# Down products of one-expert units as three rounded products, and scatters signalled by result buffer, in a hybrid trunk step with a 64-expert mixture

## The chip, the cores and the metric

One core of one Trainium2 chip. The metric is the device time of one execution of the whole program in microseconds (us), the median of several runs.

## The reference, cut to what matters

One inference step of one transformer-like layer over 384 tokens (128 context, 256 latent) of width 1024: input projections, three mixers (attention, convolution, recurrence), an output projection, and a mixture of experts. The change lies in the mixture:

```python
def moe(x, lp):
    s = jax.nn.sigmoid((x @ lp['w_router']).astype(jnp.float32))
    ...
    _, eidx = lax.top_k(jnp.where(emask, sel, NEG_BIG), TOP_K)     # 8 of 64 experts a token
    w = w / jnp.sum(w, axis=-1, keepdims=True) * ROUTED_SCALE
    ...
    hg = jnp.einsum('nd,edf->nef', x, lp['w_gate'])                # 1024 -> 256
    hu = jnp.einsum('nd,edf->nef', x, lp['w_up'])
    hid = jax.nn.silu(hg) * hu * combine[:, :, None]
    y = jnp.einsum('nef,efd->nd', hid, lp['w_down'])               # 256 -> 1024
    sh = (jax.nn.silu(x @ lp['w_sh_gate']) * (x @ lp['w_sh_up'])) @ lp['w_sh_down']
    return y + sh
```

All data are float32. Each expert has 1 MB (1024 KB) of gate weights, 1 MB of up weights and 1 MB of down weights.

## The kernel before

The program is written engine by engine: each engine has its own stream of instructions and waits on counting semaphores (`x.wait_ge(sem, n)`), which other engines' instructions or landed DMAs raise. The order of the work on every engine is thus written out by hand.

**The mixture in units.** After the router, the program makes a table of rounds. A *unit* is a pass of up to 128 token rows: either one expert with 128 rows (slots 0 and 1), or two experts with 64 rows each (slot 2, whose second expert lies in slot 3). Units come in the order one expert, one expert, two experts, and again; for these inputs there are 40, so 27 have one expert and 13 two. Their number is known only on the chip, so each engine runs a loop of `PASSES` passes over `BODY` = 12 written-out steps, each under an `If(i <= units)`. In the code, `p` is the place in the pass, `p % 3` the slot, `p % 2` the half of double buffers.

**Four weight slots** (`WSLOT`) each hold gate and up weights (`GU_W`, 128x4096) and down weights (`DN_W`, 128x2048). SyncE refills the gate and up part of a slot once the unit's gate and up products are done (`gu_ready`), the down part once its down products are (`dn_ready`), lines 658 to 663.

**A step `i`**, by engine:

- *TensorE* (lines 1995 to 2069): transposes the gathered rows of the unit after next (`transposes`, L2002), multiplies the first half of gate and up of the next unit (L2016, or L2018 and L2019 for two experts), transposes the hidden of this unit (`hidden_t`, L2051), makes the index products of a later unit (L1671), the second half of gate and up, and then this unit's down products into banks 6 and 7 of PSUM (`down`, L2033, or L2035 and L2036). Before the down products it waits for `ht_done` and `ys_done` (the banks' last content taken).
- *ScalarE* (`step`, from line 990): copies transposed rows out of PSUM (`take_xt`, L979), copies the transposed hidden (`HT`, L996), and does the silu of the next gate products (`silu`, L983).
- *VectorE* (`step`, from line 1590): makes one-hots of a later unit (L1120, L1121) and its row indices from the index products (L1130, L1131), multiplies silu and up products (`hidden`, L1577), and scales the down products by the routing weight into one of two result buffers (`YS`, L1599), for which it waits for `added`.
- *GpSimd* (`step`, from line 1074): gathers the token rows of a later unit into one of three buffers by an indirect DMA (`gather`, L1052), then writes the result rows of this unit to `y_parts` in memory by an indirect DMA (L1083), the *scatter*. Then it waits until that scatter has landed and raises `added`:

```python
indirect_dma_start(y_parts, ..., YS[:, p % 2, :], ...).then_inc(scat, 16)
pool.wait_ge(scat, 16 * i)
pool.sem_inc(added, 1)
```

Before the loop, GpSimd multiplies and adds the shared expert's outputs (`SHO`, L1069 and L1070, six operations, `sh_added`).

**After the loop** SyncE waits for all scatters and loads the parts (12 MB) back; TensorE and VectorE sum them (L2084, L1615 to L1618), with the last two results taken straight from `YS` by one-hot products (L2092, `OHT` from L1643).

**Rounded products.** Elsewhere the kernel already multiplies in the faster type fp32r: an operand is split in a high part, the value rounded to fp32r (ScalarE's copy), and a low part, the rest (VectorE's subtraction), and the product is high x high + low x high + high x low. The input projection does so (L1716 to L1718, L1737 to L1742; rounding L802 and L810, subtraction L1189 and L1220). The down products of the loop are plain float32 before the change. A name that ends in `_r` (`bigA_r`) is the same memory seen as fp32r.

## Time and profile before

| | |
|---|---|
| median of 3 runs | 1120.38 us (1119.14 to 1123.11) |
| the profiled execution | 1122.39 us |
| its span, first to last instruction | 1120.3 us |
| mean granted TensorE clock | 0.989 of full speed |
| busy share: TensorE, VectorE, ScalarE, GpSimd | 95%, 41%, 27%, 12% |
| expert loop, first gate product to last down product | 588.6 to 1076.9 us |

Times in the trace are microseconds from the span's start. PE is TensorE (PEld its weight loads), DVE VectorE, ACT ScalarE, POOL GpSimd, SP SyncE; a q behind the name is the engine's own queue. A row names line, engine, operation, output<-input, and in brackets how long the engine stood idle before it and what released it. Matmuls overlap: the time shown for one is longer than the distance from one start to the next.

### The profile page before, as it was taken

What the parts mean: (1) busy time and instruction counts of PE and PEld (TensorE: products, weight loads), DVE (VectorE), ACT (ScalarE), POOL (GpSimd) and SP (SyncE); (2) the same over time, 40 slices, a digit from 0 to 9 for tenths busy, and PEclk for the clock granted to TensorE, in tenths of its full rate; (3) what the DMA queues carried; (4) which work ended last, traced back from release to release, by engine and by line L of the source; (5) the groups of instructions that cost most, each with busy time, mean ns of one, the idle gap of its engine ahead of it and who ended that gap; (6) DMA issues with size and microseconds to landing.
All of it is one profiled execution on the core that took longest, in us unless ns stands there. A gap on an engine that the chain in (4) does not pass through costs nothing.

```text
span 1120.3 us, 14730 instructions
## 1 busy us (share of the span) xinstructions
PE 1065.5 (95%) x4768; PEld 680.4 (61%) x4768; DVE 460.8 (41%) x1056; ACT 306.7 (27%) x449; POOL 132.8 (12%) x142
## 2 busy tenths in 40 slices
PE   4899999999899999999989999999999999999985
PEld 2389888788788897965644444444444444444432
DVE  2233554445798857934722221222122212222148
ACT  3233444327444436400321111111111111111101
POOL 0020232000000000000025112111111112111100
PEclk9899999999999999999999999999999999999998
DMA  9999777446554423730279999999999999999583
GB/s 355 397 257 355 122 120 105 143 161 233 208 181 152 151 77 112 277 99 2 93 290 404 376 395 379 405 388 385 400 397 409 382 387 407 412 400 388 218 358 165
DMA packets 88527, 306.60 MB, mean 274 GB/s; under 512 B 13398, under 2 KB 17750, under 8 KB 66464
## 3 DMA queue, kind: packets, MB, share of 16 engines
q1 hardware_dynamic: 68896, 270.63, 61.9%
q0 software_dynamic: 12256, 26.80, 10.5%
q10 hardware_dynamic: 7328, 8.55, 2.2%
q8 instruction: 29, 0.48, 0.2%
q14 instruction: 18, 0.15, 0.0%
HBM read 285.31 MB, written 36.85 MB: 288 GB/s over the span
## 4 chain that ended last, share of the span: by engine, by line
PE 31%; DMA 24%; issue 6%; DVE 2%; POOLq 1%; ACT 1%; POOL 0%; DVEq 0%
DMA y_parts<-bigB,IDX 23%; PE PS L2016 4%; PE PS L1915 4%; PE PS L1662 3%; PE PS L2018 3%; PE PS L2033 3%; DMA bigB<-n_rows,IDX 2%; PE PS L1973 1%; PE PS L2084 1%; PE PS L2002 1%; PE PS L1904 1%; PE PS L1903 1%; PE PS L1905 1%; PE PS L2035 1%; PE PS L2092 1%
## 5 line engine op out<-in xcount | busy, mean ns | idle before, releaser
L2016 PE MATMUL PS<-bigB 128*128 128x512 f32 x224 | 102.3, 600 | 0.0
L1716 PE MATMUL PS<-bigB_r 128*128 128x384 f32 x288 | 98.6, 342 | 1.3 <-ACT bigB L784 1.3
L1718 PE MATMUL PS<-bigB_r,bigA_r 128*128 128x384 f32 x288 | 96.5, 335 | 0.0
L1717 PE MATMUL PS<-nT_r,bigB_r 128*128 128x384 f32 x288 | 96.3, 334 | 0.0
L2018 PE MATMUL PS<-bigA,bigB 128*64 128x512 f32 x208 | 94.8, 598 | 0.0
L2019 PE MATMUL PS<-bigB 128*64 128x512 f32 x208 | 94.8, 598 | 0.0
L2016 PE MATMUL PS<-bigA,bigB 128*128 128x512 f32 x208 | 94.6, 598 | 0.0
L1599 DVE TENSOR_SCALAR bigB<-PS,bigD 128x1024 f32<-128x1024 f32 x40 | 51.3, 1284 | 102.2 <-PE PS L2033 68.8
L979 ACT ACTIVATE bigB<-PS 128x1024 f32<-128x1024 f32 x40 | 41.0, 1025 | 158.0 <-PE PS L2002 158.0
L1220 DVE TENSOR_TENSOR bigA_r<-bigA,bigB_r 128x2048 fp32r<-128x2048 f32 x18 | 41.3, 2293 | 97.5 <-ACT bigB_r L810 97.5
L1577 DVE TENSOR_TENSOR bigB<-bigB,PS 128x256 f32<-128x256 f32 x40 | 16.9, 422 | 155.7 <-ACT bigB L983 155.7
L784 ACT ACTIVATE bigB<-PS 128x384 f32<-128x384 f32 (+1 forms) x55 | 27.3, 497 | 147.5 <-PE PS L1718 70.2
L1052 POOL DMA_INDIRECT bigB<-n_rows,IDX x27 | 27.5, 1019 | 336.7 <-issue 285.3
L1130 DVE TENSOR_REDUCE bigD<-PS 128x1 f32<-128x2 f32 (+1 forms) x58 | 9.2, 158 | 138.5 <-PE PS L1671 128.2
L2016 PEld LDWEIGHTS PS<-bigB 128*128 128x128 f32 x224 | 40.9, 192 | 41.4 <-issue 41.4
L1730 PE MATMUL PS<-bigC_r,bigA_r 128*128 128x384 f32 x192 | 65.5, 341 | 0.0
L2016 PEld LDWEIGHTS PS<-bigA,bigB 128*128 128x128 f32 x208 | 37.6, 191 | 37.3 <-issue 37.3
L1716 PEld LDWEIGHTS PS<-bigB_r 128*128 128x128 f32 x288 | 54.0, 188 | 7.3 <-issue 4.3
L983 ACT ACTIVATE bigB<-PS 128x256 f32<-128x256 f32 x40 | 15.4, 384 | 143.4 <-PE PS L2016 97.9
L2018 PEld LDWEIGHTS PS<-bigA,bigB 128*64 128x64 f32 x208 | 26.3, 136 | 46.3 <-issue 44.5
L1717 PEld LDWEIGHTS PS<-nT_r,bigB_r 128*128 128x128 f32 x288 | 54.1, 188 | 0.0
L1718 PEld LDWEIGHTS PS<-bigB_r,bigA_r 128*128 128x128 f32 x288 | 54.1, 188 | 0.0
(362 smaller groups left out, 1997.9 us busy)
## 6 DMA issues: line engine op xcount, KB each, us to landing
bigA<-in_w_in SPq DMA_DIRECT2D x17, 2048.0 KB, 11.4
bigB<-in_w_gate SPq DMA_DIRECT2D x27, 1024.0 KB, 9.3
bigB<-in_w_up SPq DMA_DIRECT2D x27, 1024.0 KB, 12.6
bigB<-in_w_down SPq DMA_DIRECT2D x27, 1024.0 KB, 11.4
bigA<-in_w_gate SPq DMA_DIRECT2D x26, 1024.0 KB
bigA<-in_w_up SPq DMA_DIRECT2D x26, 1024.0 KB
bigA<-in_w_down SPq DMA_DIRECT2D x26, 1024.0 KB
bigA<-in_w_ada SPq DMA_DIRECT2D x8, 2048.0 KB, 9.8
```

The costliest lines, as they stand in the source:

```text
L979: nc.scalar.activation(XT[:, b, :, :].rearrange("p (a k) t -> p a (k t)", a=2), PS[:, 0:2, :], ACT.Copy).then_inc(xt_done, 1)
L1220: nc.vector.tensor_tensor(low, w, WHI[:, i % 2, :, :].bitcast(F32), ALU.subtract).then_inc(wlo_done, 1)
L1599: nc.vector.tensor_scalar(YS[:, p % 2, :].rearrange("p (a n) -> p a n", a=2), PS[:, 6:8, :], WC[:, p:p + 1], None, ALU.mult).then_inc(ys_d ...
L1662: last = mm(out, lhs(k), rhs(k), start=(k == 0), stop=(k == n - 1))
L1716: mm(out, wh, nh, start=(k == 0), stop=False)
L1717: mm(out, wh, nl, start=False, stop=False)
L1718: last = mm(out, wl, nh, start=False, stop=(k == KD - 1))
L1730: last = mm(out, low[:, k, :], NHI2[:, k, :], start=False, stop=(k == KD - 1))
L1915: last = mm(PS[:, 6 + hf, :], G[:, k, m * P:(m + 1) * P], w[:, k, :], start=(k == 0), stop=(k == KD - 1))
L2016: last = mm(PS[:, 2 + b, :], XT[:, b, k, :], GU_W[s][:, :, k, :], start=first, stop=stop)
L2018: mm(PS[0:HALF, 2 + b, :], XT[:, b, k, 0:HALF], GU_W[2][:, :, k, :], start=first, stop=stop)
L2019: last = mm(PS[HALF:P, 2 + b, :], XT[:, b, k, HALF:P], GU_W[3][:, :, k, :], start=first, stop=stop)
```

## The change

1. For units of slots 0 and 1, ScalarE rounds the down weights into a new buffer `DNH` (one buffer for both slots; 8 KB a partition), and VectorE subtracts it from the weights, in place, into `DNL`. `DNH` lies where two of the shared outputs lay, so the first rounding waits for two `sh_added`; in slot 1 the rounding waits for the down products of the unit before, which read the same buffer.
2. ScalarE's copy of the transposed hidden becomes the high part (`HTH`), and VectorE makes its low part (`HTL`) out of PSUM.
3. TensorE makes three rounded products for each f32 product: 12 instructions of 512 columns instead of 8. Units with two experts stay as they are.
4. Each result buffer has its own scatter semaphore (two semaphores of the attention biases, used again, hence the offset `scat0`). VectorE waits on it before it writes the buffer again. GpSimd no longer waits after a scatter, save in the last two steps.

```diff
@@ ScalarE
+            def down_high(turn, i, s):
+                act.wait_ge(dn_loaded[s], 16 * turn)
+                if s == 0:
+                    act.wait_ge(sh_added, NT - 1)
+                else:
+                    act.wait_ge(dn_ready, i - 1)
+                nc.scalar.activation(DNH, DN_W[s], ACT.Copy).then_inc(dn_high, 1)
...
                 act.wait_ge(gu_ready, i)
+                if p % 3 < 2:
+                    down_high(pas * 4 + (p // 3 + 1), i, p % 3)
                 with act.If(i + 2 <= units):
                     take_xt(i + 1, p % 2)
                 act.wait_ge(ht_ready, i)
-                nc.scalar.activation(HT[:, p % 2, :, :], PS[:, 5, 0:2 * P].rearrange("p (k t) -> p k t", k=2),
+                nc.scalar.activation((HTH if p % 3 < 2 else HT)[:, p % 2, :, :], PS[:, 5, 0:2 * P].rearrange("p (k t) -> p k t", k=2),
@@ GpSimd
             pool.wait_ge(out_done, 96)
-            pool.sem_inc(added, 2)
...
-                                            YS[:, p % 2, :], None, bounds_check=T * TOPK - 1, oob_is_err=False).then_inc(scat, 16)
-                    pool.wait_ge(scat, 16 * i)
+                                            YS[:, p % 2, :], None, bounds_check=T * TOPK - 1,
+                                            oob_is_err=False).then_inc(scat[p % 2], 16)
+                with pool.Else():
+                    pool.wait_ge(scat[p % 2], pas * (16 * BODY // 2) + (scat0 + 16 * (p // 2)))
                     pool.sem_inc(added, 1)
@@ VectorE
+            def down_low(p):
+                if p % 3 < 2:
+                    dve.wait_ge(dn_high, pas * (BODY // 3 * 2) + (p // 3 * 2 + p % 3 + 1))
+                    nc.vector.tensor_tensor(DNL[p % 3], DN_W[p % 3], DNH.bitcast(F32), ALU.subtract).then_inc(dn_low, 1)
+
+            def hidden_low(i, p):
+                if p % 3 < 2:
+                    dve.wait_ge(ht_done, i)
+                    nc.vector.tensor_tensor(HTL[:, p % 2, :, :], PS[:, 5, 0:2 * P].rearrange("p (k t) -> p k t", k=2),
+                                            HTH[:, p % 2, :, :].bitcast(F32), ALU.subtract).then_inc(dn_low, 1)
...
                 with dve.If(i + 1 <= units):
-                    prepare(i, p)
+                    one_hots(pas * 8 + u // 3 * 2, u % 3, u % 2)
+                    down_low(p)
+                    take_index(i + AHEAD, u % BODY, u % 3)
+                    hidden_low(i, p)
                     dve.wait_ge(ht_ready, i)
                     hidden(i, (1 + p) % 2)
+                with dve.Else():
+                    down_low(p)
+                    hidden_low(i, p)
                 nc.vector.tensor_copy(TOKF[:, p % 2:p % 2 + 1], IDX[:, p, 0:1])
                 dve.wait_ge(dn_ready, i)
-                dve.wait_ge(added, i)
+                dve.wait_ge(scat[p % 2], pas * (16 * BODY // 2) + (scat0 + 16 * (p // 2)))
@@ TensorE, down(turn, p)
-                pe.wait_ge(dn_loaded[s], 16 * turn)
...
+                if s < 2:
+                    pe.wait_ge(dn_low, pas * (BODY // 3 * 4) + 2 * (p // 3 * 2 + p % 3 + 1))
+                    for hf in range(2):
+                        cols, out = slice(hf * 512, (hf + 1) * 512), PS[:, 6 + hf, :]
+                        for k in range(2):
+                            mm(out, HTH[:, b, k, :], DNH[:, k, cols], start=(k == 0), stop=False)
+                            mm(out, HTL[:, b, k, :], DNH[:, k, cols], start=False, stop=False)
+                            last = mm(out, HTH[:, b, k, :], DNL[s][:, k, cols], start=False, stop=(k == 1))
```

How the instructions stand. **ScalarE, the step of a slot-1 unit** (L979 is `take_xt`, L996 the hidden, L983 the silu), before:

```order
L993 REGISTER_ALU [waits gate_up_products]
L993 COMPARE_AND_BRANCH
L979 ACTIVATE bigB<-PS 128x1024 [waits gathered_t]
L993 UNCONDITIONAL_BRANCH
L996 ACTIVATE bigB<-PS 128x256 [waits hidden_t]
```

and with the change:

```order
L997 ISA [waits gate_up_products]
L1002 ACTIVATE bigC_r<-bigA 128x2048 [waits down_products,down_loaded_1]
L1009 REGISTER_ALU
L1009 COMPARE_AND_BRANCH
L985 ACTIVATE bigB<-PS 128x1024 [waits gathered_t]
L1009 UNCONDITIONAL_BRANCH
L1012 ACTIVATE bigB_r<-PS 128x256 [waits hidden_t]
```

The rounding of 128x2048 stands ahead of the copy of gathered rows, and its wait for down products and weights is now ScalarE's.

**VectorE, the same step** (one-hots, index, hidden, result), before:

```order
L1120 TENSOR_TENSOR bigC_r<-K,bigC 128x384
L1121 ISA
L1121 COPY bigD_r<-bigD_r 128x3x3
L1127 REGISTER_ALU
L1130 TENSOR_REDUCE bigD<-PS 128x1 [waits index_products]
L1131 TENSOR_SCALAR IDX<-PS 128x2
L1577 TENSOR_TENSOR bigB<-bigB,PS 128x256 [waits silu,hidden_t]
```

and with the change:

```order
L1137 TENSOR_TENSOR bigC_r<-K,bigC 128x384
L1138 ISA
L1138 COPY bigD_r<-bigD_r 128x3x3
L1603 REGISTER_ALU
L1604 TENSOR_TENSOR bigA_r<-bigA,bigC_r 128x2048 [waits down_w_high_ready]
L1144 REGISTER_ALU
L1147 TENSOR_REDUCE bigD<-PS 128x1 [waits index_products]
L1148 TENSOR_SCALAR IDX<-PS 128x2
L1609 TENSOR_TENSOR bigB_r<-PS,bigB_r 128x256 [waits hidden_t_taken]
L1594 TENSOR_TENSOR bigB<-bigB,PS 128x256 [waits silu,hidden_t]
```

The subtraction of the weights stands between one-hots and index, that of the hidden behind the index.

**GpSimd, one step** (gather, scatter), before:

```order
L1052 DMA bigB<-n_rows,IDX 128x1024 [waits gathered_t,indices]
L1077 UNCONDITIONAL_BRANCH
L1080 REGISTER_ALU
L1080 COMPARE_AND_BRANCH
L1081 REGISTER_ALU
L1083 DMA y_parts<-bigB,IDX 3072x1024 [waits results_weighted]
L1085 REGISTER_ALU
L1080 UNCONDITIONAL_BRANCH [waits results_added]
```

and with the change:

```order
L1068 DMA bigB<-n_rows,IDX 128x1024 [waits gathered_t,indices]
L1092 UNCONDITIONAL_BRANCH
L1095 REGISTER_ALU
L1095 COMPARE_AND_BRANCH
L1096 REGISTER_ALU
L1098 DMA y_parts<-bigB,IDX 3072x1024 [waits results_weighted]
L1095 UNCONDITIONAL_BRANCH
L1102 ISA
L1101 UNCONDITIONAL_BRANCH [waits bias_loaded_then_results_written_0]
```

The wait for the scatter is gone from the path of a step with a scatter; the one that is left stands in the other branch, which only the last two steps take.

## Rows read from the trace of the kernel before

**Rows 1.** The page: busy us (share of the span), instructions of each engine

```profile
PE 1065.5 (95%) x4768; PEld 680.4 (61%) x4768; DVE 460.8 (41%) x1056; ACT 306.7 (27%) x449; POOL 132.8 (12%) x142
```

**Rows 2.** Busy time in stretches: stretch, its length, busy (instructions) of PE, PEld, DVE, ACT, POOL; granted clock, DMA share, GB/s

```profile
692.28:728.60 36.32, 36.32 (x136) 16.68 (x135) 8.01 (x25) 5.38 (x9) 6.07 (x6) 1.00 0.98 394
...
1070.00:1085.00 15.00, 10.73 (x29) 4.16 (x26) 5.21 (x11) 0.38 (x1) 0.00 (x0) 1.00 1.01 419
```

**Rows 3.** The waits of TensorE in the expert loop: us in total, times, longest

```profile
PE PS L2002 <- DMA bigB<-n_rows,IDX: 1.9, 4, 1.2
...
PE PS L2002 <- DMA nT<-n_rows,IDX: 0.7, 1, 0.7
```

**Rows 4.** The scatter's line L1083: who waited for it, and its landings

```profile
  POOL bigB L1052: 183.4, 17
...
DMA to landing us min/median/max: 3.3/10.1/11.3
```

**Rows 5.** SyncE's issue of a down load in time, and all of them: landing

```profile
682.64 0.33 SPq L663 DMA_DIRECT2D bigB<-in_w_down  x1
...
DMA to landing us min/median/max: 5.1/11.4/14.9
```

**Rows 6.** Down products, L2033: one unit in time, and the group of the loop

```profile
714.86 3.60 PE L2033 MATMUL PS<-bigB 128*128 128x512 f32 x8
...
L2033 PE MATMUL PS<-bigB 128*128 128x512 f32 x104 | 46.8, 592 | 0.0
```

**Rows 7.** Rounded products of the same width in the input projection, in time

```profile
60.10 0.39 PE L1737 MATMUL PS<-bigB_r 128*128 128x512 f32 x1
...
61.46 1.98 PE L1742 MATMUL PS<-bigB_r,nT_r 128*128 128x512 f32 x8
```

**Rows 8.** ScalarE's rounding and VectorE's subtraction in the projections: ns min/median/max

```profile
L810 ACT ACTIVATE bigB_r<-bigA x18: 1903/1908/1921, 64.0 to 259.5; 128x2048 fp32r<-128x2048 f32 x18
...
L1220 DVE TENSOR_TENSOR bigA_r<-bigA,bigB_r x18: 2291/2293/2294, 65.9 to 261.5; 128x2048 fp32r<-128x2048 f32 x18
```

**Rows 9.** One step of ScalarE and VectorE in time

```profile
703.01 0.38 ACT L983 ACTIVATE bigB<-PS 128x256 f32<-128x256 f32 x1 [3.45 <-PE PS L2016]
...
706.54 1.28 DVE L1599 TENSOR_SCALAR bigB<-PS,bigD 128x1024 f32<-128x1024 f32 x1 [2.56 <-PE PS L2036]
...
708.35 0.16 DVE L1121 CAST bigD_r<-bigD_r 128x9 fp32r x1
...
711.29 0.38 ACT L996 ACTIVATE bigB<-PS 128x256 f32<-128x256 f32 x1 [2.64 <-PE PS L2051]
```

**Rows 10.** The end of the loop in time: a gather, its reader, the next reader

```profile
1026.82 1.02 POOL L1052 DMA_INDIRECT nT<-n_rows,IDX  x1 [11.00 <-issue]
...
1034.75 1.15 PE L2002 MATMUL PS<-K,nT 128*128 128x128 f32 x8 [0.66 <-DMA nT<-n_rows,IDX]
...
1047.96 1.16 PE L2002 MATMUL PS<-K,bigB 128*128 128x128 f32 x8 [1.20 <-DMA bigB<-n_rows,IDX]
```

**Rows 11.** The start of the loop in time: GpSimd, VectorE, first down products

```profile
599.04 2.34 POOL L1070 TENSOR_TENSOR bigB<-bigB,nT 128x1024 f32<-128x1024 f32 x1
...
599.10 2.31 DVE L1121 CAST bigD_r<-bigD_r 128x9 fp32r x1
...
605.75 3.60 PE L2033 MATMUL PS<-bigB 128*128 128x512 f32 x8
```

**Rows 12.** The last steps and the merge in time

```profile
1071.66 1.28 DVE L1599 TENSOR_SCALAR bigB<-PS,bigD 128x1024 f32<-128x1024 f32 x1 [2.56 <-PE PS L2036]
...
1073.19 3.69 PE L2033 MATMUL PS<-bigB 128*128 128x512 f32 x8 [1.14 <-DVE bigB L1599]
...
1083.71 7.13 PE L2092 MATMUL PS<-bigB,bigC 128*128 128x512 f32 x16 [0.40 <-DVE bigC L1643]
```

**Rows 13.** GpSimd's issue beside a VectorE operation, in time

```profile
634.84 1.02 POOL L1052 DMA_INDIRECT bigB<-n_rows,IDX  x1 [9.93 <-PE PS L2002]
...
634.86 0.37 DVE L1120 TENSOR_TENSOR bigC_r<-K,bigC 128x192 fp32r<-128x192 f32 x1
```

More of the change, by code:

```diff
@@ L351, in trunk @@
         HT = cut(bigB, 8704, (2, 2, P))
+        HTH = cut(bigB_r, 8704, (2, 2, P))
+        HTL = cut(bigB_r, 12288, (2, 2, P))
+        DNH = cut(bigC_r, 0, (2, D))
+        DNL = [cut(bigB_r, 4096, (2, D)), cut(bigA_r, 10240, (2, D))]
         SHO = [bigC[:, 0:D], bigC[:, D:2 * D], nT_flat[:, 2 * D:3 * D]]
@@ L400, in trunk @@
         in_state = sem("state_loaded")
-        in_bias = [sem("bias_loaded_0"), sem("bias_loaded_1")]
+        in_bias = [sem("bias_loaded_then_results_written_0"), sem("bias_loaded_then_results_written_1")]
         bias_masked = sem("bias_masked")
@@ L472, in trunk @@
         rows_go = sem("row_transfer_may_start")
-        added = sem("results_added_through")
+        added = sem("all_results_written")
         sh_loaded = sem("shared_weights_loaded")
@@ L519, in trunk @@
         ht_done = sem("hidden_t_taken")
+        dn_high = sem("down_w_high_ready")
+        dn_low = sem("down_w_low_then_hidden_low_ready")
         dn_ready = sem("down_products")
         ys_done = sem("results_weighted")
-        scat = sem("results_added")
+        scat, scat0 = in_bias, 64 * (NH // 2)
         y_back = [sem(f"early_ada_then_parts_loaded_{m}") for m in range(4 * NT)]
@@ L692, in _ @@
             sp.wait_ge(sh_added, NT)
-            sp.wait_ge(added, units)
+            sp.wait_ge(added, 2)
             parts = y_parts.rearrange("(m p r) d -> m p r d", p=P, r=TOPK)
@@ L2025, in down @@
                 b, s = p % 2, p % 3
-                pe.wait_ge(dn_loaded[s], 16 * turn)
-                if s == 2:
-                    pe.wait_ge(dn_loaded[3], 16 * turn)
+                if s < 2:
[6 more added lines that the diff above has]
+                            last = mm(out, HTH[:, b, k, :], DNL[s][:, k, cols], start=False, stop=(k == 1))
+                    last.then_inc(dn_ready, 1)
+                    return
+                pe.wait_ge(dn_loaded[2], 16 * turn)
+                pe.wait_ge(dn_loaded[3], 16 * turn)
                 for hf in range(2):
@@ L2031, in down @@
                     for k in range(2):
-                        if s < 2:
-                            last = mm(PS[:, 6 + hf, :], HT[:, b, k, :], DN_W[s][:, k, cols], start=(k == 0), stop=(k == 1))
-                        else:
-                            mm(PS[0:HALF, 6 + hf, :], HT[:, b, k, 0:HALF], DN_W[2][:, k, cols], start=(k == 0), stop=(k == 1))
-                            last = mm(PS[HALF:P, 6 + hf, :], HT[:, b, k, HALF:P], DN_W[3][:, k, cols], start=(k == 0), stop=(k == 1))
+                        mm(PS[0:HALF, 6 + hf, :], HT[:, b, k, 0:HALF], DN_W[2][:, k, cols], start=(k == 0), stop=(k == 1))
+                        last = mm(PS[HALF:P, 6 + hf, :], HT[:, b, k, HALF:P], DN_W[3][:, k, cols], start=(k == 0), stop=(k == 1))
                 last.then_inc(dn_ready, 1)
```

5 lines of the change are left out of this document (1 added, 4 removed).

## The prediction

> **What bounds the kernel now.** The page first: TensorE is busy for 95% of the span [rows 1]. Next, busy time in stretches over the expert loop. Its 40 units come as one-expert, one-expert, two-expert, and three of them take 36.3 us; in [rows 2] TensorE is busy in all 36.32 us of such a stretch, at a granted clock of 1.00 (its 2.4 GHz level), and the DMA engines are busy too: share 0.98 at 394 GB/s. Who is the limit is told by the waits of TensorE: in 475 us it waited for no weights at all, and 1.9 + 0.7 us for gathered rows [rows 3]. So TensorE sets the pace, two others close behind. One is GpSimd: it issues a scatter, waits for its landing (10.1 us in the median), and only then issues the next gather; that wait held back the gathers of one buffer pair for 183.4 us [rows 4]. This loop takes about as long as a unit (12.1 us), so it must go if TensorE is to be quicker. The other is the transfer of weights. A one-expert unit's down weights are issued at 682.64 and land 11.4 us later in the median, 14.9 at most [rows 5]; TensorE reads them at 714.86 [rows 6].
>
> **The products.** A one-expert unit's down products are 8 f32 matmul instructions of 512 columns: 3.60 us for eight, each shown as 0.59, so one starts every (3.60 - 0.59) / 7 = 0.430 us, 3.44 us in all [rows 6]. The change makes them 12 rounded ones. Their pace stands in the input projection, where the kernel does the same trick at the same width: eight in 1.98 us, each shown as 0.39, so (1.98 - 0.39) / 7 = 0.227 us [rows 7], with a weight load before each, as here. 12 x 0.227 = 2.72 us. A unit saves 0.72 us, and 27 of the 40 units have one expert: **-19.3 us**, all of it on TensorE, which has no other idle time to hide it.
>
> **The high and low parts.** ScalarE copies 128x2048 weights into rounded form: 1.91 us; VectorE subtracts over the same size: 2.29 us [rows 8]. A third operation, 128x256 from PSUM, I take as the 0.42 us of the `hidden` product of that size in the code, with 0.16 of the smallest operation [rows 9] and 1.15, half the 2048-column one, as bounds. I follow the step whose down products start at 714.86 [rows 9]. ScalarE is free after the silu at 703.01 and, in the slot-0 turn, waits for no earlier product: the copy ends at about 705.4, before anything else of ScalarE is due. VectorE scales the previous result from 706.54 to 707.8, makes the one-hots until 708.5, and subtracts until 710.8. Only then does the hidden transposed come out of ScalarE, 711.29 + 0.4 = 711.7; with four index operations of 0.16 ahead of it on VectorE, its low part is done at about 712.4. TensorE wants it at 714.86: 2.4 us to spare. In the slot-1 turn the copy must wait for the previous down products (shared buffer), but there is only one one-hot operation and a two-expert unit on TensorE: spare 3 us by the same count. So the extra 4.6 us of ScalarE and VectorE per unit cost **0**; the cover is TensorE's gate and up products, and without it (last step, below) they cost. In the order, the copy of the next unit's gathered rows stands behind ScalarE's new copy; it ends some 1 us later in the slot-1 turn and is wanted in the next step: 0. The down weights are now wanted when gate and up end (about 702.8), not at 714.86: 702.8 - 682.64 = 20.2 us after issue against 11.4 (14.9 at most) to land [rows 5]: 9 us to spare, 5 in the worst case. 0, but this is the new narrow place.
>
> **GpSimd and the scatters.** The wait goes from GpSimd to VectorE, which asks for the scatter of two units before (24 us old against 10.1 to land [rows 4]): 0. GpSimd then issues scatter and next gather back to back, so a gather starts a landing, some 10 us, earlier. Near the end one issued at 1026.82 was read at 1034.75, 7.9 us later, and TensorE stood 0.66 us before it, 1.20 before the next [rows 10]. All such waits go: **-2.6 us**, the sum of [rows 3]. Bounds: 0 and -4, one more late gather's 1.20 us beyond the sum.
>
> **The start.** ScalarE's first copy waits until GpSimd has done two of its three shared additions. The last addition starts at 599.04 and each operation takes 2.3 [rows 11], so the second is done at 596.7 and the copy at 598.7. VectorE leaves its one-hots only at about 601.7 (a copy of it ends at 601.4), so by the count above the low parts are ready at 605.3; TensorE starts these products at 605.75 [rows 11]. **0**, bounds 0 and +1.
>
> **The last step.** Here nothing covers. VectorE scales the last but one result until 1072.9, and only then may subtract: 1072.9 + 0.1 + 2.29 + 0.42 + waits = 1075.9, where the down products now start at 1073.19 [rows 12]: 2.7 us later. They are 0.7 us shorter, so **+2.0 us**. The merge behind it starts at 1083.71, by VectorE's one-hots after its last scaling, and TensorE is then busy to the end of its part; the delay passes on in full. Bounds 0 and +2.7.
>
> **Sum.** The profiled execution took 1122.4 us (span 1120.3), 2.0 over the median of 1120.4. -19.3 - 2.6 + 2.0 = -19.9: 1102.5 for it, **1100.5 us** against the median. Does DMA allow it? The stretch of [rows 2] moved 36.32 us x 394 GB/s = 14.3 MB. Flat out the engines gave 419 GB/s at share 1.01, in reads of partial results [rows 2]: 34.1 us. TensorE will want 36.3 - 2 x 0.72 = 34.9. It fits by 2%.
>
> **Rivals.**
> (a) *DMA becomes the bound.* For: share is 0.98 already, and the writes and gathers are slower than plain reads. If 394 GB/s is all this mix gives, the stretch stays 36.3 and each of some 12 falls 1.4 us behind, 17 in all; the landing of down weights has 9 us to spare before ScalarE stands, so some 8 are lost: 1109. Against: 419 in [rows 2]. Beside this stands the Trainium skill (DMA: Bandwidth & Descriptors, Where 436 GB/s comes from), which lets HBM give a core some 358 GB/s where the pair shares it; by that the loop could not be as fast as it is, and the 394 and 419 measured here decide against it.
> (b) *VectorE and GpSimd block each other.* At the start VectorE's tiny copy took 2.31 us beside GpSimd's addition of 2.34, and ended with it [rows 11]; elsewhere it takes 0.16 [rows 9]. GpSimd's two issues of 1.0 us [rows 13] now fall just where the subtraction starts. If both held it up, with 0.6 us of sequencing around them (an estimate), it would be 2.6 us late, 0.2 over the spare of the 14 slot-0 units, and the start 1 more: 1104. Against: at 634.86 a VectorE operation with both inputs in SBUF took its usual 0.37 beside a GpSimd issue [rows 13]. The Trainium skill (SBUF — State Buffer, Who interferes with whom) has such a two-input operation contend with GpSimd's reads; rows 11 agree for additions, rows 13 don't for issues.
> (c) *Slower: the low parts come late in every step.* The point is 2.4 us of spare plus the 0.72 gained: a VectorE chain 3.1 us longer than I count. If the copy or the subtraction queued as in the last step, each unit would lose 2.7 - 0.7 = 2.0 us, 27 x 2 = 54: 1172. Against: only the last step lacks TensorE work between.
> (d) *The change doesn't do what it says*: the wait on scatters still paces, now at VectorE, since two may be under way. Then a unit stays near 12.1 us: 1119. Against: a buffer has two steps, 24 us, for a landing of 10.
>
> **How the numbers follow.** Chances: my forecast 0.78, with its own range from 1097.5 (all of the 4 us from gathers, a mild last step) to 1104; (a) 0.11; (b) 0.03; (c) 0.04; (d) 0.04. The range 1097 to 1109 takes (a) and (b) in and leaves (c), (d) out. A measurement of this kernel tells 0.3%, 3.4 us, from no change. Faster by more: 0.91 (forecast, nearly all of a and b); within: 0.04 (d); slower: 0.05.
>
> **What would show it.** Twelve rounded matmuls in 2.7 us behind the gate and up products; three units in 34.9 us; TensorE idle nowhere but at the last step, 2.7 us longer there; the subtraction done before the index products return; GpSimd's gathers within 2 us of each scaled result; DMA share near 1.0 and 410 GB/s, landings later by no more than some us. Wrong would be: TensorE or ScalarE waiting for down weights (a); a subtraction over 3 us (b); TensorE waiting for VectorE ahead of the down products (c).

## The result, and the profile after

| | before | changed |
|---|---|---|
| median, us | 1123.11 of 5 runs (1119.14 to 1127.12) | 1110.58 of 5 runs (1105.11 to 1111.01) |
| ratio | | 0.988, 95% interval 0.985 to 0.991 |
| the profiled execution, its span | 1122.39, 1120.3 | 1105.11, 1103.3 |
| busy share: TensorE, VectorE, ScalarE, GpSimd | 95%, 41%, 27%, 12% | 95%, 48%, 32%, 15% |

The change is worth 1.2%, some 13 us, where 20 were forecast, and 1110.58 lies outside the range of 1097 to 1109. The profiled execution is the fastest of the five; the section on experiments comes back to that. The three runs of the kernel before that stood at hand had a median of 1120.4; with the later ones it is 1122 to 1123.

First the page of the changed kernel, to be read beside [rows 1]:

```profile
PE 1046.7 (95%) x4876; PEld 702.0 (64%) x4876; DVE 531.1 (48%) x1110; ACT 355.2 (32%) x476; POOL 166.0 (15%) x142
```

TensorE is busy for 18.8 us less with 108 instructions more (27 units, 12 instead of 8). Its waits from 590 to 1065 us (columns: line, releaser, us in total, times, longest), to be read beside [rows 3]:

```profile
PE PS L2060 <- DVE bigB_r L1609: 3.6, 1, 3.6
PE PS L2047 <- issue: 3.3, 2, 2.1
PE PS L2119 <- issue: 1.8, 1, 1.8
PE PS L1700 <- DVE bigD_r L1138: 1.1, 1, 1.1
```

The waits for gathered rows are gone. L2119 is the merge, whose first wait took 2.7 us before (L2084), behind the end of [rows 3]; L1700 has the same wait for one-hots as before, 1.1 us. Two kinds are new: 3.6 us ahead of the last down products (L2060), forecast at 2.7 more than the 1.14 there before, and 3.3 us ahead of gate and up products of two-expert units (L2047). The name "issue" says that the trace has no releaser for them. It is a load, as the rows in time show: SyncE's two up loads for the unit, and TensorE's first product on them.

```profile
966.56 0.38 SPq L665 DMA_DIRECT2D bigA<-in_w_up  x1
...
968.22 0.39 SPq L665 DMA_DIRECT2D bigB<-in_w_up  x1
...
994.34 0.61 PE L2047 MATMUL PS<-bigA,bigB 128*64 128x512 f32 x1 [2.12 <-issue]
```

The second was issued at 968.22 and took the longest of its line, 26.0 us, so it landed at 994.2, just ahead of the product that waited. Here are the landings of the up loads (L665) and of the down loads (L669), from 640 to 1050:

```profile
DMA to landing us min/median/max: 9.9/18.4/26.0
...
DMA to landing us min/median/max: 13.5/19.4/27.2
```

Down loads took 11.4 us in the median before [rows 5], and 19.4 now; up loads 12.6 before, and 18.4 now. Busy time in stretches of 35 us, columns as in [rows 2], tells the rest:

```profile
690.00:725.00 35.00, 35.00 (x144) 18.26 (x144) 13.29 (x29) 9.01 (x11) 9.82 (x6) 1.00 1.01 411
...
900.00:935.00 35.00, 35.00 (x145) 18.34 (x144) 13.14 (x29) 8.98 (x11) 8.04 (x7) 1.00 1.01 415
935.00:970.00 35.00, 33.85 (x142) 17.95 (x141) 13.15 (x29) 8.80 (x11) 6.34 (x6) 1.00 0.99 408
970.00:1005.00 35.00, 32.88 (x133) 16.98 (x132) 11.42 (x28) 7.80 (x11) 6.05 (x6) 1.00 0.96 396
```

DMA is at a share of 1.00 to 1.01 from 690 to 935 and moves 405 to 416 GB/s. TensorE is busy in all of that time, then stands for 1.15 and 2.12 us. How can a stream that falls behind its reader leave it busy to 935? By its lead. I took for each two-expert unit (units counted from 0) the time from the landing of its last gate or up load to its first product: 11.2 us at unit 5, 8.8, 7.9, 7.0, 5.8, 5.0, 4.7, 3.7 and 1.7 at every third unit behind it, and 0.1 at units 32, 35 and 38. Before the change it lies between 10.6 and 14.6 from unit 5 on, mostly at 12 to 13, and shows no trend. With the change the lead shrinks by about 1 us in three units and is used up at unit 32.

Last, the last step, in time:

```profile
1051.33 1.28 DVE L1628 TENSOR_SCALAR bigB<-PS,bigD 128x1024 f32<-128x1024 f32 x1 [2.67 <-PE PS L2071]
...
1052.54 2.28 DVE L1604 TENSOR_TENSOR bigB_r<-bigB,bigC_r 128x2048 fp32r<-128x2048 f32 x1
1054.73 0.42 DVE L1609 TENSOR_TENSOR bigB_r<-PS,bigB_r 128x256 fp32r<-128x256 f32 x1
...
1055.20 0.79 PE L2060 MATMUL PS<-bigC_r,bigB_r 128*128 128x512 f32 x1 [3.59 <-DVE bigB_r L1609]
1055.80 0.63 PE L2061 MATMUL PS<-bigC_r,bigB_r 128*128 128x512 f32 x1
1056.22 0.63 PE L2062 MATMUL PS<-bigB_r 128*128 128x512 f32 x1
...
1066.66 3.70 PE L2127 MATMUL PS<-bigB,bigC 128*128 128x512 f32 x8 [1.48 <-DVE bigC L1672]
```

The chain scaling, subtraction, hidden low part is as forecast. The products behind it are not: they start 0.43 us apart instead of 0.23. The stretch from 1055.0 tells why, its last three columns being granted clock, DMA share and GB/s:

```profile
1055.00:1058.40 3.40, 3.20 (x8) 2.52 (x9) 0.21 (x2) 0.00 (x0) 0.00 (x0) 0.50 1.01 426
```

TensorE had stood 3.59 us, and its clock was at the lower of its two levels, 1.2 GHz, for 3.4 us behind that.

The account of the two spans, 1120.3 and 1103.3 us, from the starts of products:

| stretch | before | changed | difference |
|---|---|---|---|
| to the first gate product of the loop | 588.6 | 586.3 | -2.3 |
| from there to the last but one down products | 479.4 | 461.2 | -18.1 |
| the last step, from there to the merge's L2127 (L2092 before) | 15.76 | 19.13 | +3.4 |
| the rest | 36.6 | 36.6 | 0 |

The change has no part in the first row. In the second, three units take 34.89 us where nothing stops TensorE, and 36.23 before: a one-expert unit saves 0.67 us, the 26 in this row 17.4. The stops for weights make two groups of three units longer (36.10 and 37.08 us), +3.5 in all. The waits for gathered rows had made groups before longer, by 3.9 us in all, with what goes on around them, of which [rows 3] has 2.6. A rest of -0.3 has no name. Without the first row the change is -14.8.

### The profile page after: what moved, and what is told of

It reads as the page before. It is cut to its first block, busy times and chain, and to the rows that moved or that the text cites. A ratio compares the mean times of both kernels' runs of the same rounds, so it can differ in the third digit from the quotient of the medians.

```text
span 1103.3 us, 15100 instructions
## 1 busy us (share of the span) xinstructions
PE 1046.7 (95%) x4876; PEld 702.0 (64%) x4876; DVE 531.1 (48%) x1110; ACT 355.2 (32%) x476; POOL 166.0 (15%) x142
## 4 chain that ended last, share of the span: by engine, by line
PE 60%; DVE 2%; issue 1%; ACT 1%; DVEq 0%
PE PS L2045 17%; PE PS L2047 8%; PE PS L2070 4%; PE PS L1944 4%; PE PS L2031 3%; PE PS L1691 3%; PE PS L2060 3%; PE PS L2062 2%; PE PS L2061 2%; PE PS L2002 1%; PE PS L2119 1%; PE PS L2086 1%; PE PS L1932 1%; PE PS L1933 1%; PE PS L1934 1%
## 5 line engine op out<-in xcount | busy, mean ns | idle before, releaser
L1098 POOL DMA_INDIRECT y_parts<-bigB,IDX x38 | 72.3, 1902 | 323.8 <-DVE bigB L1628 314.7
L2045 PE MATMUL PS<-bigB 128*128 128x512 f32 x224 | 102.3, 600 | 0.0
L2047 PE MATMUL PS<-bigA,bigB 128*64 128x512 f32 x208 | 94.7, 598 | 3.3 <-issue 3.3
L2045 PE MATMUL PS<-bigA,bigB 128*128 128x512 f32 x208 | 94.6, 597 | 0.0
L1594 DVE TENSOR_TENSOR bigB<-bigB,PS 128x256 f32<-128x256 f32 x40 | 16.9, 422 | 134.3 <-ACT bigB L989 134.3
L2045 PEld LDWEIGHTS PS<-bigB 128*128 128x128 f32 x224 | 40.9, 192 | 41.0 <-issue 40.9
L2045 PEld LDWEIGHTS PS<-bigA,bigB 128*128 128x128 f32 x208 | 37.5, 191 | 37.3 <-issue 37.3
L2047 PEld LDWEIGHTS PS<-bigA,bigB 128*64 128x64 f32 x208 | 26.3, 136 | 49.2 <-issue 47.8
L2060 PE MATMUL PS<-bigC_r,bigB_r 128*128 128x512 f32 x108 | 49.8, 461 | 3.6 <-DVE bigB_r L1609 3.6
## 6 DMA issues: line engine op xcount, KB each, us to landing
bigA<-in_w_down SPq DMA_DIRECT2D x26, 1024.0 KB, 19.2
```

What stands on the lines that cost most here:

```text
L1098: pool.indirect_dma_start(y_parts, bass.IndirectOffsetOnAxis(ap=IDX[:, p, 1:2], axis=0), YS[:, p % 2, :], None, bounds_check=T * TOPK - 1, ...
L2045: last = mm(PS[:, 2 + b, :], XT[:, b, k, :], GU_W[s][:, :, k, :], start=first, stop=stop)
L2047: mm(PS[0:HALF, 2 + b, :], XT[:, b, k, 0:HALF], GU_W[2][:, :, k, :], start=first, stop=stop)
L2060: mm(out, HTH[:, b, k, :], DNH[:, k, cols], start=(k == 0), stop=False)
```

## The experiments

Eleven kernels ran, each beside the kernel before on the same chip. Ratios are to its runs.

**Run e1: the changed kernel again**, as it is.

> The changed kernel unaltered, for a second trace: the first profiled execution took 1105.1 us, four others 1110.3 to 1111.0 at a granted clock of 0.984 to 0.985 instead of 0.989. Theory (the weight stream has become the limit): an execution of 1110 shows down weights landing later than 20 us after issue, margins of the gate and up loads gone before unit 32, and 8 to 10 us of TensorE idle in the last third of the loop instead of 3.5, with stretches at half clock behind those stops. Rival (the extra time has another place, before the loop or in VectorE and GpSimd blocking each other): the loop takes 469 us as in the first trace and the difference stands elsewhere.

Measured: 1108.44 us (1105.73 to 1113.63), ratio 0.987, 0.984 to 0.991. Its waits:

```profile
PE PS L2060 <- DVE bigB_r L1609: 3.9, 2, 3.6
PE PS L2047 <- issue: 2.8, 2, 2.6
PE PS L2119 <- issue: 1.8, 1, 1.8
```

The size of the effect, the stops for weights and the one in the last step come again, so they do not belong to one execution alone. The 8 to 10 us of stops that the theory asked for in an execution of 1110 us are not there, but this one took 1106.4: no profile shows the changed kernel at 1110. From the first gate product to the last down product (start to start) it is 473.1 us here and 473.0 in the first profile, and 487.7 before. What differs between executions are stretches of 3.4 us at half clock: 5 before the end of the merge in the first profile, 8 in this one, 4 to 9 in the profiles of this case (run e4 has more). Each costs 1.7 us where TensorE works all through it, so they can account for a spread of some 8 us, which both kernels have; that they do was not measured execution by execution.

**Run e2: the products alone.**

```diff
-                                            oob_is_err=False).then_inc(scat[p % 2], 16)
+                                            oob_is_err=False).then_inc(scat, 16)
+                    pool.wait_ge(scat, 16 * i)
...
-                dve.wait_ge(scat[p % 2], pas * (16 * BODY // 2) + (scat0 + 16 * (p // 2)))
+                dve.wait_ge(added, i)
```

> The rounded products, but the scatters as before: one semaphore, GpSimd waits for each landing before the next gather. Theory: GpSimd's serial loop, about 12.1 us a unit with a landing of 10.1, then sets the pace, gathers come late from the first units on, TensorE waits 0.5 us and more in each step before its transposes, and the time is within 5 us of the kernel before (ratio 0.995 to 1.005). Rival (the serial loop has slack and the rounded products alone bring the gain): ratio as for the whole change, 0.988.

Measured: 1128.24 us (1125.12 to 1132.62), ratio 1.004, 1.002 to 1.007: slower than before the change. The waits of TensorE:

```profile
PE PS L2031 <- DMA bigB<-n_rows,IDX: 16.9, 12, 1.9
```

TensorE's work is as short as with the whole change, and 16.9 us come back as waits for gathered rows, against 2.6 in [rows 3]. The loop through GpSimd (scatter, its landing, next gather) takes longer than the quicker unit, as the prediction said of it. From the two-expert unit 2 to unit 38 (twelve groups of three units) it takes 439.1 us, before the change 438.7, and with the whole change 422.2. The last step is 3.3 us longer than before, as in the changed kernel, and the profiled execution had the slower start described below; it is slower than the kernel before by these two. How many of the other executions had that start is not known.

**Run e3: the scatters alone**, with the products in float32 as before.

> The scatters signalled by result buffer, the products plain float32. Theory: only TensorE's waits for gathered rows go, 2.6 us: ratio 0.998 (0.996 to 1.000); GpSimd's issue of a scatter stays at 1.0 us, since no subtraction stands beside it on VectorE. Rival (the wait on scatters was the real bound, and its removal brings most of the gain): ratio 0.99 or less.

Measured: 1117.65 us (1116.38 to 1123.98), ratio 0.996, 0.993 to 0.999, some 5 us less than before where 2.6 were expected; the interval holds both. TensorE waits for no gathered row, and all twelve groups of three units take 36.23 us, 434.8 in all: 3.9 less than before. The two parts alone are +0.4% and -0.4%; together they are -1.2%. That is more than their sum: the second part is what lets the first one through.

**Run e4: half of the up weights.**

```diff
-                sp.dma_start(WSLOT[q][:, KD * DE:2 * KD * DE], flat(wu)).then_inc(gu_loaded[q], 16)
+                sp.dma_start(WSLOT[q][0:rows, KD * DE:2 * KD * DE], flat(wu)[0:rows, :]).then_inc(gu_loaded[q], 16)
...
-                                gate_up_of(r, q)
+                                gate_up_of(r, q, HALF)
```

> The changed kernel with half of each expert's up weights (64 of 128 partitions) not loaded from unit 3 on, so these keep an older expert's rows and the output is not the reference's: 0.5 of 3 MB less per expert, some 15% less to move, everything else equal. Theory (weight stream is the limit late in the loop): no TensorE wait but the first steps' and the last step's, landings near 10 us throughout, ratio 0.983 to 0.985 against the kernel before (3.5 us less than the changed kernel's first trace, 9 less than its slower ones), and little spread between runs. Rival (the stops of TensorE come from somewhere else): as the changed kernel, 0.988.

Measured: 1248.15 us, ratio 1.112. This was to lighten DMA and did the opposite. A stretch of 100 us, columns as above:

```profile
690.00:790.00 100.00, 79.61 (x290) 39.91 (x288) 26.13 (x58) 17.38 (x22) 12.10 (x12) 0.89 1.02 263
```

The share is 1.02, yet only 263 GB/s are moved. In this mix the loads of 64 partitions kept the engines at least as busy as those of 128 had. The run says nothing on the theory, except that with a slow stream TensorE's waits are those of L2047 again (68.0 us), with 21.3 at L2060 and 14.5 at L2045. The next run takes away whole loads instead.

**Run e5: one load in twelve less.**

```diff
-                                gate_up_of(r, q)
+                                gate_up_of(r, q, 1 if q == 3 else P)
```

> The changed kernel with 1 MB of 12 less to load in every three units: inside the loop the up weights of the second expert of a two-expert unit are not loaded, save one partition of 128 (so that part of the result is of the expert before). All other loads keep their 128 partitions, and every semaphore is raised as before. Theory (the stream of weights can't quite keep up with the quicker TensorE, and its lead of some 12 us is used up over 30 units): with 8% less to move the lead no longer shrinks; the margin between a gate and up load's landing and its first product stays near 10 us to the end of the loop, the stops of TensorE for weights (3.3 and 2.8 us in the two profiles of the changed kernel) go to 0, landings of the down loads fall from 19 us in the median to some 12. Time 1107, 3.5 under the changed kernel, ratio to the kernel before 0.984 to 0.986. Rival (the 5 us missed lie elsewhere, in half-clock windows around the loop or in the merge): landings may shorten, the time stays at 1110, ratio 0.988.

Measured: 1107.42 us (1101.11 to 1109.65), ratio 0.985, 0.982 to 0.988. All the waits of TensorE from 590 to 1075:

```profile
PE PS L2060 <- DVE bigB_r L1609: 3.6, 1, 3.6
PE PS L2119 <- issue: 3.2, 1, 3.2
PE PS L1700 <- DVE bigD_r L1138: 2.6, 1, 2.6
```

No stop for weights is left. Two stretches, the first and the last of nine:

```profile
690.00:725.00 35.00, 35.00 (x145) 18.25 (x143) 13.28 (x29) 9.00 (x11) 9.82 (x6) 1.00 0.96 379
...
970.00:1005.00 35.00, 35.00 (x146) 18.32 (x145) 13.40 (x30) 9.01 (x11) 9.83 (x6) 1.00 0.97 395
```

TensorE is busy for all 315 us of the nine. The lead at two-expert units stays between 17.3 and 18.8 us from unit 5 to the end, and the median landing of a down load is 10.6 us. The time is 1 to 3 us under the changed kernel (its two sets of runs) where 3.5 were expected, and the intervals overlap, so the time alone shows no gain; what the run settles is the mechanism: less to move, and the lead no longer shrinks.

**Run e6: the same load left out of the kernel before.**

> The same load left out of the kernel before the change (inside the loop, up weights of the second expert of a two-expert unit, 127 of 128 partitions not loaded). Theory: there TensorE alone is the bound, it never waits for weights, so nothing is won: ratio 1.000, at most 1 us by chance. If this kernel too became faster by over 3 us, the stream would already have been a bound before the change, and the shrinking lead would not be the change's doing.

Measured: 1120.30 us (1113.76 to 1126.23), ratio 0.998, 0.996 to 1.001. The lead at two-expert units is 19 to 20 us near the end, and TensorE waits for no weights. So before the change the stream was no bound that a lighter load could lift (the interval allows 5 us at most).

**Run e7: the subtraction a step earlier.**

```diff
                     one_hots(pas * 8 + u // 3 * 2, u % 3, u % 2)
-                    down_low(p)
+                    if p % 3 == 1:
+                        down_low(p)
...
                     hidden(i, (1 + p) % 2)
+                    if p % 3 == 2:
+                        down_low(p + 1)
```

> The changed kernel, but VectorE subtracts the high part of the down weights of a slot-0 unit in the step before (of the two-expert unit ahead of it), behind the hidden product and ahead of scaling that unit's result, so that in the last step the subtraction runs beside TensorE's down products. Theory (the last step's delay is VectorE's chain scaling, subtraction, hidden low part): the scaling moves 1.2 us later behind the subtraction, which takes 2.3 us off the chain; TensorE's idle time ahead of the last down products falls from 3.6 us to about 2.5. If the half clock behind it comes of an idle time of 3.6 us, it may go too, 1.4 us more. Time 1 to 2.5 us under the changed kernel: 1108.5, ratio 0.986 to 0.987. Rival (the chain of the last step is set by another engine, ScalarE's copy of the hidden or the scatter): idle time stays 3.6, ratio 0.988. Risk: 13 scalings come 1.2 us later, which nobody waits for before 8 us later: 0.

Measured: 1110.95 us (1102.36 to 1116.49), ratio 0.990, 0.987 to 0.993: no gain shown. The waits of TensorE:

```profile
PE PS L1710 <- DVE bigD_r L1138: 5.5, 3, 3.4
PE PS L2070 <- DVE bigB_r L1609: 2.3, 1, 2.3
```

The wait of the last step falls from 3.6 to 2.3 us, as expected; the clock is half behind it all the same (1052.2 to 1055.6). What I called a risk of 0 is the first line: index products wait for VectorE's one-hots, 3.4 us once. The rows before that wait:

```profile
983.34 1.27 DVE L1638 TENSOR_SCALAR bigB<-PS,bigD 128x1024 f32<-128x1024 f32 x1
...
985.43 0.49 PE L1710 MATMUL PS<-bigD_r,bigC_r 128*128 128x8 f32 x3 [3.35 <-DVE bigD_r L1138]
```

Between 640 and 1050 us VectorE waited for ScalarE's rounding 26.7 us in 12 times ahead of slot-0 subtractions. In the changed kernel that was 2.5 us (ahead of slot-1 subtractions it is the other way round, 16.0 there and 5.0 here). The rounding itself waits for down weights, which come late when the stream is slow. The edit moved a late load onto VectorE, and everything behind it on that engine (the scaling, then the one-hots) came late too. So the cover of the down weights, which I had called the new narrow place, is real; the changed kernel has it in the one spot where nobody waits behind.

**Run e8: the last unit in float32.**

```diff
@@ TensorE, down
+                if s < 2 and last_unit:
+                    pe.wait_ge(dn_loaded[s], 16 * turn)
+                    for hf in range(2):
+                        last = product(PS[:, 6 + hf, :], lambda k: HT[:, b, k, :], lambda k: DN_W[s][:, k, hf * 512:(hf + 1) * 512], 2)
+                    last.then_inc(dn_ready, 1)
+                    return
@@ VectorE
-                with dve.Else():
-                    down_low(p)
-                    hidden_low(i, p)
@@ ScalarE
+                with act.Else():
+                    act.wait_ge(ht_ready, i)
+                    hidden_of(HT)
```

> The changed kernel, but the last unit keeps its down products in float32 (eight instructions, no rounding of its weights, no subtractions), each engine taking another branch in the last step. Theory: the last step goes back to what it was before the change: TensorE idle ahead of the last down products 1.1 us instead of 3.6, no half clock behind it, first merge product 15.8 us after the start of the last but one down products instead of 19.1. Time 3.3 us under the changed kernel: 1107.3, ratio 0.985 to 0.986; the rest of the loop as in the changed kernel, its stops for weights included. Rival (the merge waits for something else, such as the partial results' loads, which start with the last scatters): under 1 us won, ratio 0.988.

Measured: 1107.44 us (1103.00 to 1110.74), ratio 0.986, 0.983 to 0.989; 1 to 3 us under the changed kernel, with intervals that overlap. The last step:

```profile
1054.29 0.64 PE L2077 MATMUL PS<-bigA,bigB 128*64 128x512 f32 x1
...
1059.63 3.70 PE L1692 MATMUL PS<-bigB 128*128 128x512 f32 x8 [1.25 <-DVE bigB L1629]
...
1070.92 7.03 PE L2137 MATMUL PS<-bigB,bigC 128*128 128x512 f32 x16
```

TensorE stands 1.25 us instead of 3.59, eight products of 0.43 follow at full clock, and the merge's L2137 starts 16.63 us after the last but one down products, against 19.13. Ahead of the remaining 0.9 over the old 15.76 stands a stretch at half clock in the merge (1065.6 to 1069.0); run e11, which has the same edit and no such stretch, takes 16.00.

**The start.** The profiles show two kinds of start of the loop: a quick one (before, the first of the changed kernel, runs e1, e3, e6 and e7) and a slow one (runs e2, e4, e5 and e8). In run e5:

```profile
596.66 2.36 POOL L1085 TENSOR_TENSOR nT<-nT,bigC 128x1024 f32<-128x1024 f32 x1
596.80 2.44 DVE L1137 TENSOR_TENSOR bigC_r<-K,bigC 128x192 fp32r<-128x192 f32 x1 [1.17 <-issue]
...
599.10 2.34 POOL L1086 TENSOR_TENSOR bigB<-bigB,nT 128x1024 f32<-128x1024 f32 x1
599.16 2.31 DVE L1138 CAST bigD_r<-bigD_r 128x9 fp32r x1
...
601.94 0.80 PE L1700 MATMUL PS<-bigD_r,bigC_r 128*128 128x8 f32 x3 [2.62 <-DVE bigD_r L1138]
```

VectorE's one-hots end only with GpSimd's last addition, and TensorE waits 2.62 us for them; then its clock is half for 6.8 us. In the changed kernel's first profile the clock is half from 584.0 to 587.4, into the first gate products; TensorE comes 0.6 us before the end of GpSimd's last addition instead of 2.1, waits 1.08, and keeps its full clock. From the first gate product to the second unit's silu it is 17.4 us there, and 21.5 in run e5. Part of that is only where one starts to count, since the half clock also delays the first gate product: from the first transposes of gathered rows (L2031) it is 21.9 against 25.0. Three runs put this to the test, all with VectorE making these one-hots before the loop:

```diff
             take_index(AHEAD, AHEAD, AHEAD % 3)
+            one_hots((AHEAD + 1) // 3 * 2, (AHEAD + 1) % 3, (AHEAD + 1) % 2)
             hidden(0, 0)
...
-                    one_hots(pas * 8 + u // 3 * 2, u % 3, u % 2)
+                    if p > 0:
+                        one_hots(pas * 8 + u // 3 * 2, u % 3, u % 2)
+                    else:
+                        with dve.If(i >= 2):
+                            one_hots(pas * 8 + u // 3 * 2, u % 3, u % 2)
```

**Run e9: in the changed kernel.**

> The changed kernel, but VectorE makes the one-hots that step 1 of the loop used to make before the loop, where it stands idle for 7 us ahead of the first hidden product. Seven profiles so far fall in two kinds of start. Where the clock is half for part of the first unit's gate and up products (before, the changed kernel and its second run, e3, e6, e7), TensorE waits 1.1 us or less for these one-hots, which VectorE can't finish while GpSimd adds the shared outputs. Where these products run at full clock all through (e2, e5, e8), TensorE comes earlier, waits 2.6 us, and the clock is then half for 6.8 us; the silu of the second unit comes 21.5 us after the first gate product instead of 17.4. Theory (this slower start is in the four timed runs of the changed kernel near 1110.6 and not in its profile of 1105.1, and makes up the rest of my miss): with the wait gone both kinds of start vanish, the silu of the second unit comes 16.3 us after the first gate product, the median falls by some 3 us to 1107, ratio 0.985 to 0.986. Rival (the spread of the runs comes from half-clock windows elsewhere): the wait goes, the median falls by 1.1 us at most, ratio 0.988.

Measured: 1108.56 us (1103.05 to 1110.74), ratio 0.987, 0.984 to 0.990. The wait is gone, and the silu comes 15.5 us after the first gate product, in a profile whose clock is full there. But:

```profile
PE PS L2052 <- issue: 4.4, 3, 2.2
```

The stops for weights rose from 3.3 to 4.4 us. The loop is 472.1 us long against 473.0: of 1.9 us won at the start, half was given back at units 32 to 38. The theory asked for a median of 1107, the rival for one that falls by 1.1 us; 1108.56 is between them, and the intervals hold both.

**Run e10: in the kernel before.**

> The same edit in the kernel before the change. Theory: its code at the start is the same, so it has the same two kinds of start, and gains as much: 3 us, ratio 0.997. If it gains 1 us or nothing while the changed kernel gains 3 or more, the slower start comes mostly with the change, and the term I set at 0 for the start was wrong by the difference.

Measured: 1121.05 us (1118.62 to 1124.07), ratio 0.998, 0.996 to 1.001: 1 us won, or 2, or none. The edit is worth 0 to 2 us in either kernel. That the slower start comes with the change is neither shown nor excluded: of the profiles without this edit, the three with float32 products (before, e3, e6) have the quick start, and four of the seven with rounded ones (e2, e4, e5, e8) the slow one.

**Run e11: both mends.**

> Both mends together: one-hots of step 1 ahead of the loop, and the last unit's down products in float32 as in e8. Theory: the gains add, 3 and 2 to 3 us under the changed kernel: 1104.5, ratio 0.983; the stops for late weights (some 3 us at units 32 to 38) stay, and come a little earlier, since the loop starts sooner and the stream does not. Rival: the sooner start is given back at these stops in full, since the transfer of weights sets the end of the loop: 1107.4 as e8, ratio 0.986.

Measured: 1104.61 us (1099.22 to 1106.02), ratio 0.983, 0.980 to 0.986, as expected and 4 us under run e9 on the same chip. The waits of TensorE:

```profile
PE PS L2053 <- issue: 4.6, 3, 2.2
PE PS L2134 <- issue: 2.5, 1, 2.5
PE PS L1697 <- DVE bigB L1634: 1.2, 1, 1.2
```

This is the fastest kernel of the study, and what it still waits for in the loop is the stream of weights. From the first gate product to the last down product it takes 469.1 us, and its clock is full from 294 to 1092 us.

## Why the prediction was wrong

- **The products**, -19.3: right in kind, and near in size. Twelve instructions 0.23 us apart; three units take 34.89 us (forecast 34.9). But without its waits the kernel before took 36.23, not 36.3, so a unit saves 0.67 us and not 0.716: 17.4 us in the 26 units ahead of the last, where the forecast has 18.6. Its sum also counts the last unit's 0.7 us twice, in these 19.3 and in the +2.0 of the last step: by its own terms it should have read -19.2 and not -19.9.
- **The high and low parts**, 0: right, and so was the narrow place. ScalarE's rounding takes 1.91 us, the subtraction 2.28, the hidden's low part 0.42, and the low parts are there before TensorE wants them in every step but the last (in run e1 it waits 0.3 us once more). From unit 25 on ScalarE waits for down weights, 41.7 us in nine times; TensorE does not. Run e7 shows that VectorE can be made to feel it.
- **GpSimd and the scatters**, -2.6: right in kind; by the length of the groups it is -3.9 (run e3), inside the bounds. The text undersold it: without it the first part is lost (run e2).
- **The start**, 0: the trace after has the same wait as before, 1.1 us. Other executions have a slower start; whether it comes with the change is open (run e10).
- **The last step**, +2.0: this term was mis-sized, it is +3.4. The wait was right (+2.4 of 2.7). Left out was the half clock behind it, though the profile before has stretches at half clock: from the first of the twelve products to the last it takes 4.12 us (1055.20 to 1059.32), and 2.63 in run e5, where the clock is full: 1.5 us. The same stop stands in five profiles of kernels with this last step (3.5 to 3.6 us); the clock is half at once behind four of them, and 5 us later in run e5. Run e8 takes wait and clock away together.
- **"It fits by 2%"**: this step failed. It set 419 GB/s, the rate of plain reads of partial results, against a demand of 14.3 MB in 34.9 us, 410 GB/s. With the change the mix of the loop, with its gathers and scatters, gave 405 to 416 at a share of 1.00 to 1.01, on average about 412; and the 14.3 MB were of one stretch. Eleven such stretches of the kernel before move 14.4 MB on average, late ones more, two of them 14.7 and 14.5 (columns as in [rows 2]):

```profile
910.30:947.00 36.70, 36.70 (x137) 16.95 (x136) 8.00 (x25) 5.38 (x9) 6.06 (x6) 1.00 0.99 400
947.00:983.20 36.20, 36.20 (x136) 16.77 (x135) 8.00 (x25) 5.38 (x9) 6.29 (x6) 1.00 1.00 401
```

14.4 MB in 34.9 us is 412 GB/s, all that the mix gave, and 14.7 is 421: nothing was left over. Loads landed later, the lead of 11 us went by 1 us in three units, and +3.5 us of stops came at the end; runs e5 and e6 show it from both sides. How large the shortfall is does not follow from these rates: they differ by less than 1%, while the lead goes by 3% of the time. What makes the rest of it stays open. Rival (a) had this mechanism, with the rate too low (394, that of a stream that had pauses) and hence 8 us lost. The trace of before held the sharper sign: a share of 0.98 to 1.00 with a TensorE that is about to ask for 4% more.
- **The other rivals.** (b) fell as it was put: no subtraction of the changed kernel takes over 2.3 us; what is held up is GpSimd, at no cost (below). Its 0.6 us of sequencing stood on no row, and its rows 11 show a cast, which has one input; the operation with two inputs beside it (L1120, at 598.27) took 0.90 us instead of 0.34. (c): TensorE waits for low parts in the last step, and hardly elsewhere. (d): no wait on a scatter shows on VectorE.
- **The base.** I took 2.0 us off the profiled execution, to meet a median of three runs. Over 62 runs of the kernel before in four sets the medians are 1122.1 to 1123.3, so the profiled 1122.4 was the better base, and the subtraction put 2 to 3 us of error into the number.

So from the corrected -19.2: 1.2 us less from the products, 1.3 more from the gathers, 3.5 of stops, 1.4 more in the last step (1.5 of half clock, little else), and the rest of 0.3, which makes the -14.8 us of the account, but for rounding. The measured ratios, 0.988 and 0.987, are -13 and -15 with intervals of some 3 us either way. The 2.6 us between forecast (1102.5) and profiled execution (1105.1) looked small only because that execution's loop happened to start 2.3 us early. Whether a rest of 1 or 2 us in the median belongs to something else, such as a slower start that is more frequent with the change, stays open: run e10 neither shows nor excludes it.

## What to carry to other kernels

Where two engines are both near 100%, ask of the one that is not yet the bound what it can give for this mix of transfers, not for its best kind, and take its load from many stretches, not one. A margin of 2% is none. A stream that falls behind uses up its lead first, here 11 us at 1 us in three units, so that the stops begin 30 units on; read the lead in two places of the trace, since mean rates need not show the loss. A wait moved off an engine may be worth little by itself (0.4%) and still be the condition for the rest (run e2 against the changed kernel), so cost the parts together. And a stop of TensorE can cost more than its length, where the clock is half behind it: put that in the bounds, and look whether the last pass of a loop, where nothing covers, should stay as it was (run e8).

## What the runs showed of the hardware

**GpSimd's issue is held up by VectorE's subtraction**, not the other way round. In the changed kernel:

```profile
747.95 2.29 DVE L1604 TENSOR_TENSOR bigA_r<-bigA,bigC_r 128x2048 fp32r<-128x2048 f32 x1
748.22 2.90 POOL L1098 DMA_INDIRECT y_parts<-bigB,IDX  x1 [7.10 <-DVE bigB L1628]
```

A scatter's issue that starts when the subtraction is under way takes 2.90 us, and the subtraction keeps its 2.29; one that started 0.09 us ahead of a subtraction (946.25) took 1.00. In run e3, without subtractions, all 38 issues take 0.98 to 1.02. The Trainium skill (SBUF — State Buffer, Who interferes with whom) has a VectorE operation with two inputs in SBUF contend with a GpSimd instruction that reads SBUF, but infers that such an operation leaves GpSimd's generation of DMA descriptors alone. The trace does not agree with that inference: the issue is held up, by 1.9 us a time. It cost nothing here: the next gather came at 751.43, and none was late.

**Fewer bytes in a narrower load did not relieve the stream** (run e4): with 64 of 128 partitions in one load of three, it moved 263 GB/s at full share, against 412; with a whole load in twelve left out but for one partition (run e5), the share fell to 0.94 to 0.98.

**Half clock does not follow every stop.** In the profiles of this case but run e4's, TensorE stands 23 times for 2 us or more behind the loop's first gate product; in 13 of these cases the clock is half where it goes on or within 2 us of that, in 10 it is not (3.59 us in the last step here: half; 3.35 us at 985 in run e7: full).

**Half clock can save time.** An execution whose clock is half early, up to the loop's first products, reaches a wait that ends with GpSimd's last addition later against it, stands less, and kept its clock: 21.9 us from the first transposes to the second silu, against 25.0 in one at full clock. All six quick and all four slow starts of the unedited loop have this pattern; no run changed the clock alone.
